# Scan of a two-block transformer kernel: the time steps are multiplied into the decay matrices on GpSimd

## The reference

```python
xc = (x.astype(f32) * dt[..., None]).reshape(b, nc, SSD_CHUNK, g, r, p)
cs = jnp.cumsum((dt * a.astype(f32)).reshape(b, nc, SSD_CHUNK, g, r), axis=2)
...
seg = cs[:, :, :, None] - cs[:, :, None, :]
lower = jnp.tril(jnp.ones((SSD_CHUNK, SSD_CHUNK), dtype=bool))[:, :, None, None]
lmat = jnp.exp(jnp.where(lower, seg, -jnp.inf))
cb = jnp.einsum('bclgn,bcsgn->bclsg', cc, bc)
y = (jnp.einsum('bclsg,bclsgr,bcsgrp->bclgrp', cb, lmat, xc)
     + jnp.einsum('bclgn,bcgrpn,bclgr->bclgrp', cc, h_in, jnp.exp(cs)))
```

## Time and profile before

| | us |
|---|---|
| median of 3 runs | 3024.29 (3024.07 to 3032.86) |
| span of the profiled execution, first to last instruction | 3023.4 |
| TensorE busy | 2960.7 (98%) |
| VectorE busy | 1376.5 (46%) |
| GpSimd busy | 869.7 (29%) |
| ScalarE busy | 802.6 (27%) |

### The profile page before, as it was taken

The page is one execution under the profiler, slowest core; times in us unless marked ns, Lnnn a source line. Parts: engine busy times, 40 slices in busy tenths (PEclk is TensorE's granted clock), DMA queues, the critical chain, the costliest instruction groups (busy, mean ns, idle before and its releaser), DMA issues.

```text
span 3023.4 us, 38857 instructions
## 1 busy us (share of the span) xinstructions
PE 2960.7 (98%) x15464; PEld 2267.7 (75%) x15464; DVE 1376.5 (46%) x2609; ACT 802.6 (27%) x1751; POOL 869.7 (29%) x772
## 2 busy tenths in 40 slices
PE   8999999999999999999999999999998999999999
PEld 7776799998855545555558788888886666678998
DVE  1243267812265736555543533342236555541651
ACT  1022222201022325555620110110104355540210
POOL 0000234574400101221234334443230111110786
PEclk9999999999999999999999999999999999999999
DMA  7455434442345132223212122222331323234443
GB/s 258 151 202 210 147 140 164 157 168 84 126 181 221 44 112 99 84 98 108 88 70 84 70 84 86 96 84 84 112 112 42 116 102 112 105 112 153 154 168 112
DMA packets 65561, 370.18 MB, mean 122 GB/s; under 512 B 6298, under 2 KB 21722, under 8 KB 23152
## 3 DMA queue, kind: packets, MB, share of 16 engines
q1 hardware_dynamic: 49120, 334.60, 30.6%
q10 hardware_dynamic: 15296, 29.56, 2.9%
q0 software_dynamic: 976, 3.63, 0.3%
HBM read 362.30 MB, written 1.28 MB: 120 GB/s over the span
## 4 chain that ended last, share of the span: by engine, by line
PE 89%; DVE 6%; PEld 2%; ACT 1%; issue 1%; PEldq 0%; POOL 0%; DMA 0%; POOLq 0%; SPq 0%; DVEq 0%; ACTq 0%
PE PB L482 15%; PE PB L1361 13%; PE PA L482 11%; PE PS L482 8%; PE PB L362 8%; PE PB L1342 6%; PE PB L1076 5%; PE PB L1192 4%; PE PB L1375 3%; PE PB L406 2%; PE PA L1444 2%; PE PA L1413 1%; PE PA L1427 1%; DVE work L2607 1%; PE PB L1245 1%
## 5 line engine op out<-in xcount | busy, mean ns | idle before, releaser
L1361 PE MATMUL PB<-H,ring 128*128 128x512 f32 (+1 forms) x1024 | 428.1, 566 | 0.0
L1361 PEld LDWEIGHTS PB<-H,ring 128*128 128x128 f32 x1024 | 192.0, 190 | 184.4 <-issue 179.0
L517 POOL TENSOR_TENSOR sums<-ring 128x512 f32<-128x512 f32 x115 | 151.0, 1313 | 617.5 <-PE PA L482 247.5
L482 PE MATMUL PB<-work,sums 128*128 128x128 f32 (+1 forms) x1360 | 230.6, 327 | 0.0
L482 PEld LDWEIGHTS PB<-work,sums 128*128 128x128 f32 x1360 | 207.1, 191 | 17.4
L2861 POOL TENSOR_TENSOR work<-work 128x256 f32<-128x256 f32 x96 | 59.7, 642 | 519.0 <-ACT work L1867 417.0
L482 PE MATMUL PA<-work,sums 128*128 128x128 f32 (+1 forms) x1280 | 208.9, 318 | 0.0
L482 PEld LDWEIGHTS PA<-work,sums 128*128 128x128 f32 x1280 | 187.5, 191 | 13.5
L2521 DVE SCALAR_TENSOR_TENSOR work<-PB,par,work 128x510 f32<-128x510 f32 (+3 forms) x256 | 181.7, 713 | 24.1 <-ACT work L1845 17.3
L626 DVE TENSOR_TENSOR work<-PA,work 128x128 f32<-128x128 f32 (+1 forms) x53 | 18.9, 357 | 379.9 <-ACT work L610 379.9
L1342 PE MATMUL PB<-H,ring 128*128 128x512 f32 (+1 forms) x512 | 175.5, 493 | 0.0
(11 more groups left out here) (394 smaller groups left out, 5305.1 us busy)
## 6 DMA issues: line engine op xcount, KB each, us to landing
ring<-stream SPq DMA_DIRECT2D x314, 1024.0 KB, 4.8
sums<-cs_rows ACTq DMA_DIRECT2D x16, 1024.0 KB, 4.7
sums<-cs_rows ACTq DMA_DIRECT2D x16, 512.0 KB, 3.8
work<-work ACTq DMA_DIRECT2D x16, 256.0 KB, 4.5
work<-scratch POOLq DMA_DIRECT2D x1, 2560.0 KB, 13.5
X<-xT SPq DMA_DIRECT2D x2, 512.0 KB, 5.5
ring<-stream SPq DMA_DIRECT2D x2, 512.0 KB, 6.8
X<-xT SPq DMA_DIRECT2D x1, 1024.0 KB, 20.0
```

The lines of the kernel that those rows point to most:

```text
L482: mm = pe.matmul(fast_bank(side, bank)[:, col:col + width], weight(k), right(4 * part + k), start=first and opens and k == 0, stop=last an ...
L517: nc.gpsimd.tensor_tensor(su[:, 0], a21, a22, ALU.add).then_inc(sem("w_summed"), 1)
L1361: mm = pe.matmul(PB[:, pair, t, 0:Tc], ring[:, c % SLOTS, k, t * P:(t + 1) * P], H[:, k, 0:Tc], start=(k == 0), stop=(k == KT - 1))
```

## The change

`within` uses x itself, without the time steps, and one matrix per head for both directions. The time steps go into the decay matrices: when a unit's `MB` is masked, GpSimd multiplies each direction's half in place by the time steps (two instructions of 128 x 512), waits for both, and adds the two halves into a new buffer `MS[n % 2]` (one instruction of 128 x 512). TensorE then waits for this sum (`s_both`) and does four products a unit instead of eight, with pieces of `XG` as weights. `XC` is gone. `MB` now comes free when the addition has read it; `XG` comes free when TensorE's last unit of the group is done. The core of the diff:

```diff
-        XC = [area(at + 512 * i, 2, 2, 2, HD) for i in range(2)]
+        MS = [area(at + 512 * i, 2, 2 * P) for i in range(2)]
...
-                        pe.wait_ge(sem("s_m"), LAYER["s_m"] * la + n + 1)
-                        pe.wait_ge(sem("s_xc"), LAYER["s_xc"] * la + 2 * n + 2)
+                        pe.wait_ge(sem("s_both"), LAYER["s_both"] * la + n + 1)
                         for t in range(2):
                             cols = slice((t0 + t) * P, (t0 + t + 1) * P)
-                            for d in range(2):
-                                for r in range(2):
-                                    mm = pe.matmul(PA[q][HD * r:HD * r + HD, cols], XC[n % 2][:, d, t, r, :],
-                                                   MB[n % 2][:, r, d, t, :], start=(d == 0), stop=(d == 1),
-                                                   skip_group_check=True)
+                            for r in range(2):
+                                at_ = P * q + HD * r
+                                mm = pe.matmul(PA[q][HD * r:HD * r + HD, cols], XG[:, t0 + t, at_:at_ + HD],
+                                               MS[n % 2][:, r, t * P:(t + 1) * P], start=True, stop=True,
+                                               skip_group_check=True)
                         mm.then_inc(sem("s_within"), 1)
...
-                            act.wait_ge(sem("s_xc"), LAYER["s_xc"] * la + 2 * len(units) * g)
+                            act.wait_ge(sem("s_within"), LAYER["s_within"] * la + len(units) * g)
...
-                        act.wait_ge(sem("s_within"), LAYER["s_within"] * la + n - 1)
+                        act.wait_ge(sem("s_both"), LAYER["s_both"] * la + n - 1)
...
                         if n >= 2:
                             pool.wait_ge(sem("s_within"), LAYER["s_within"] * la + n - 1)
+                        pool.wait_ge(sem("s_m"), LAYER["s_m"] * la + n + 1)
+                        m = MB[n % 2].rearrange("p r d t n -> p r d (t n)")
                         for d in range(2):
                             hh = 32 * d + 4 * g + 2 * q
-                            gp.tensor_tensor(XC[n % 2][:, d, :, :, :],
-                                             XG[:, t0:t0 + 2, P * q:P * q + P].rearrange("p t (r n) -> p t r n", r=2),
-                                             DT[:, t0:t0 + 2, hh:hh + 2].unsqueeze(3).broadcast_to([P, 2, 2, HD]), ALU.mult)\
-                                .then_inc(sem("s_xc"), 1)
+                            md = MB[n % 2][:, :, d, :, :]
+                            dt_ = DT[:, t0:t0 + 2, hh:hh + 2].rearrange("p t r -> p r t").unsqueeze(3).broadcast_to([P, 2, 2, P])
+                            gp.tensor_tensor(md, md, dt_, ALU.mult).then_inc(sem("s_timed"), 1)
+                        pool.wait_ge(sem("s_timed"), LAYER["s_timed"] * la + 2 * n + 2)
+                        gp.tensor_tensor(MS[n % 2], m[:, :, 0, :], m[:, :, 1, :], ALU.add).then_inc(sem("s_both"), 1)
                         if u == len(units) // 2 - 1 and g >= 1:
                             squares(g - 1)
```

More of the change, by code:

```diff
@@ L275, in program @@
             "s_cb": 8, "s_turned": 24, "s_xd": 48, "s_delta": 48, "s_state": 48, "s_inter": 48,
-            "s_inter_read": 48, "s_cbm": 16, "s_bc": 64, "s_exp": 32, "s_fall": 32, "s_m": 32, "s_xc": 64, "s_rows": 16, "s_z": 8, "s_gain": 8, "s_sum": 8,
-            "s_within": 32, "s_mid": 32,
+            "s_inter_read": 48, "s_cbm": 16, "s_bc": 64, "s_exp": 32, "s_fall": 32, "s_m": 32, "s_rows": 16, "s_z": 8, "s_gain": 8, "s_sum": 8,
+            "s_within": 32, "s_mid": 32, "s_both": 32, "s_timed": 64,
             "z_sum": 1, "z_root": 1, "mixed": 8,
```

## The result

| | before | changed |
|---|---|---|
| median of 20 runs, us | 3024.67 | 3031.09 |
| ratio of the changed kernel to the one before | | 1.0023, interval 1.0014 to 1.0031 |
| span of the profiled execution, us | 3023.4 | 3034.5 |
| mean granted clock of TensorE in it | 0.997 | 0.992 |

The change costs 6.4 us where 38 were forecast. The time lies inside the forecast range and is slower, as forecast, but it is near rival 2 (3026), not near the forecast (3062). In some executions of every kernel, the one before too, the time is 6 to 12 us longer, so the fastest executions are compared as well: 3023.6 before, 3030.0 after.

The account below looks back on a forecast made before the run. It took TensorE to bound the kernel, other engines costing nothing if they deliver in time. 3024.3 - 24.5 (bursts) + 50.2 (waits and restarts) + 12 (clock) = 3062 us, range 3026 to 3080.

Parts of the forecast that it names:

- rival 2: Scan: VectorE is not pushed back, only GpSimd pays where the two meet; 3026 us, chance 0.10.
- Which engine sets the end, and where: Scan: TensorE alone before; then it waits for GpSimd's addition, some 4 us at unit 2 in groups 1 to 6.
- Term 1: TensorE's 48 bursts in `within`: half the products save 0.51 us each (bounds 0.42 and 0.57), 24.5 us.
- Term 2: Both layers' scans: TensorE's waits for GpSimd's addition, plus 0.25 us per restarted burst, add 50.2 us.
- the wait of 3.9 us at unit 2: Layer 0, middle groups: unit 2's sum done at 1315.5, wanted by TensorE at 1311.65.
- Term 3: TensorE's clock falls behind seven long waits of layer 0, 1.7 us each (bounds 0 and 3.4): +12 us.
- Rival 1: Scan: TensorE's clock stays up, so only bursts, waits and restarts count; 3050 us, chance 0.28.
- rival 4: TensorE's bursts don't shrink, waits shrink by up to 1 us; 3074 us, chance 0.05.
- rival 3: Scan: engines run beside each other at full speed, unit 2 is 1.1 us late; 3015 us, chance 0.06.
- Rival 5: TensorE's clock falls for 6.8 us behind every wait, layer 1's too, costing 39 us; 3089 us, chance 0.07.

Follow-up runs that it names:

- squares_first: Changed kernel with the previous group's squares moved in front of each group's first unit on GpSimd; fastest 3013.0 us, ratio 0.9967.
- half_products: Kernel before the change, with the second direction's products left out of the part within a chunk; fastest 3003.5 us, ratio 0.9935.
- longer_wait: Changed kernel with one more 128 x 1024 GpSimd instruction in unit 2 of groups 2 to 6 of layer 0; fastest 3046.7 us, ratio 1.0073.
- filler: Changed kernel with two unused TensorE products before the wait at unit 2, groups 2 to 7 of layer 0; fastest 3024.0 us, ratio 1.0008.
- again: Changed kernel run and profiled a second time without any edit; fastest 3030.4 us, ratio 1.0023.
- mask_early: Changed kernel with VectorE masking unit 1 of layer 1 before the taps; fastest 3040.5 us, ratio 1.0050.
- best: Changed kernel with the edits of squares_first and mask_early together; fastest 3025.8 us, ratio 1.0004.
- squares_split: As squares_first, but in group 7 of layer 0 the squares stand behind the first unit; fastest 3014.4 us, ratio 0.9954.
- double_products: Changed kernel with TensorE doing each of a unit's four products twice; fastest 3036.8 us, ratio 1.0040.
- best2: As best, but the squares of group 6 of layer 0 come behind the last unit of group 7; fastest 3029.9 us, ratio 1.0012.

## Why the prediction was wrong, point by point

*Which engine sets the end, and where.* Right. In the middle groups TensorE alone set it before, and the new wait is GpSimd's addition at unit 2 of groups 2 to 6, at unit 1 in layer 1, and twice in each group 7, with the squares and the masking in the chain. The forecast had group 1 among them too. squares_first shows that the squares make the wait of layer 0.

*Term 1, the bursts: 24.5 us.* Measured 20.6 (0.59 for 1.02 us) and, by half_products, 20.4. The lower bound, 0.42, was nearly the right value: a fixed part stays. The gain was 4 us smaller than forecast.

*Term 2, the waits and restarts: 50.2 us.* **This is the step that failed, in size.** Measured 20.0 us of waits and 0.07 us for each of 17 restarts (the extra time of a burst that starts from a wait), 21.2 in all, where 45 us and 0.25 stood. For the wait of 3.9 us at unit 2, the measured chain (1.74) shows where it went:
- A multiplication of 512 columns takes 1.05 us, not 1.22. I doubled the 0.61 us of 256 columns and with it the fixed part. In rows that I had, additions go from 0.72 us for 256 to 1.26 for 512, less than double; the multiplications do too. A unit takes 2.06 + 0.07 + 1.27 = 3.4 us, not 3.8, and two of them stand in the chain: 0.8 us.
- I let the masking of unit 3 in ahead of unit 2's addition, for 0.8 us. The addition started first (1263.40, the masking at 1263.69), so the masking waited and took 2.05 us, at no cost. In longer_wait, where the masking comes first, the addition pays.
- The rest, 0.5 us, is first VectorE pushed back less than I took: the masking of unit 1 began at 1252.99 in a group that began at 1223.03, which is 1301.8 on the clock of the earlier trace rows, where I had 1302.3. And TensorE comes 0.15 us later than I had it (at 1262.97, which is 1311.8 on that clock), since its bursts take 0.59 us and not 0.51.

These readings are from one trace; no run changes one of the prices alone. Group 1 was priced like groups 2 to 6, with two squares, and has one: 0.41 us for 3.9. In the last groups 2.96 and 2.50 us of waits stand where I had 5.2 and 3.6. In layer 1 the shorter unit (0.4 us) and a masking that began 0.5 us earlier than I had it made 0.79 us of the 1.75. That the two engines hold each other up is confirmed: L2572 took 1.04 us for 0.42, L2582 up to 2.05 for 1.22. It was no mistake to price it, only to let the one at unit 2's addition fall on GpSimd.

*Term 3, the clock: 12 us.* The price was right for the wait that the forecast had, but that wait did not come; measured are 3.4 to 5.0 us in the scan. Behind waits of 4.6 us the clock fell five times out of five (longer_wait), each time for 3.4 us and 1.7 us lost, the price that I took. Behind waits of 1.75 us it fell in two of the five groups in each of two profiles, and in one of them once more, behind the 2.50 us of group 7. filler shows that these falls carry the loss: without them the changed kernel stands at 3024.0. The Trainium skill (TensorE: Matmul & The Clock Gate, "Why this matters for your kernels") warns of gaps clearly longer than 1.75 us. Here the falls behind 1.75 us show that shorter ones, in otherwise dense work, can be enough, and those behind 4.6 us agree with the page.

*The sum with measured terms*, from the fastest execution before: 3023.9 - 20.6 + 20.0 + 1.2 (17 restarts) = 3024.5 without falls, where filler is (3024.0). With three falls in the scan (5.0) and the one at 2812 us (1.1) it is 3030.6, and the profiled execution of `again` took 3030.35. Behind the scan the code is the same. The profiles of `again`, `longer_wait`, `mask_early`, `best` and `squares_split` have a fall at that place; the others, those of the kernel before and the first of the changed one among them, don't. Whether the change has a part in it stays open.

*Rivals.* Rival 2's number was nearest, and that was luck: VectorE was pushed back (its masking of unit 1 began at 1301.8 for 1301.14), and of the 6 us that the kernel lost the clock had nearly all, which rival 2 leaves out. Rival 1 (the clock stays up) is out by the falls and by filler, rival 4 (no shorter burst) by half_products. The point from which rival 3 decides, a wait of 1.8 us per group, is where the kernel stands: that is why it comes out even.

*Slips in the working*, none of which decides anything. Six times 2.11 us is 12.7 and not 12.9. Rival 5 lets the clock fall for 6.8 us behind every wait, but prices the nine of layer 1 at 1.7 us where 3.4 follows; its sum would be 3104. And the 0.9 us between span and median compares two executions: in every execution listed the time is 1.9 us above the span of the same one.

## What to carry to other kernels

When work moves from a critical engine to a mostly idle one, look at the order of the idle engine's list first: 2.6 us of squares in the middle of a group decided between 11 us faster and 6 us slower, and they had cost nothing while the list had slack. A wait that the saved work has paid for is not free on TensorE if the clock can fall behind it; filling it with useless products gave those 5 to 6 us back. And price an instruction of twice the size from two sizes in the trace, never by doubling one.

## What the runs showed of the hardware

- GpSimd, fp32, two inputs in SBUF, in the traces of the kernel before, the changed one and longer_wait: 0.72 us for an addition of 256 columns and 1.26 for 512; with one operand broadcast along the columns 0.61 for 256 and 1.05 for 512 (1.89 for 1024). The broadcast form is cheaper by a sixth.
- A VectorE instruction and a GpSimd one, both with two SBUF inputs, took turns where they met, and the one that started later was the longer: masking 2.05 us for 1.22 behind the addition, addition 2.13 us for 1.27 behind the masking (longer_wait).
- The length of a wait alone did not decide whether the clock fell. Behind 0.88 us there was no fall in five (double_products). Behind 1.75 us, in the same place of equal groups, there were two in five in each of three profiles: groups 4 and 6 in the first, 3 and 5 in again and mask_early. Behind the 2.0 to 2.07 us of layer 1 in mask_early, best and best2 there were three in 21, behind the 2.50 us of group 7 two in four (again and mask_early, not the first profile nor longer_wait), behind 4.6 us five in five.
- In the first profile TensorE ran at 1.2 GHz for 20.5 us in front of the scan, while busy 20.10 of 20.50 us, and lost 9.4 us there. The profiles of double_products, best2 and squares_split have the same stretch, those of the kernel before and of the other seven runs don't. What decides it stays open.
